# Mixing layer: other block order, selection and softmax by token half between the projection blocks, branches merged block by block

## The reference, cut to what matters

```
proj = rms_norm(h) @ w_in                                  # 1024 x 4808
(q_a, k_a, v_a, q_i, k_i, w_i, gate_b, gate_c, conv_in, g_a, g_b) = split(proj)
    # widths 512, 64, 64, 512, 64, 8, 512, 512, 512, 1024, 1024
q_a, k_a, q_i, k_i = rope(...)                             # 8 heads of 64, one key head each
raw   = einsum(q_i, k_i) * 64 ** -0.5
score = einsum(relu(raw), w_i * 8 ** -0.5); score = -inf where key > query
sel   = top_k(score, 64)                                   # 64 keys per query
p     = softmax(q_a . k_a[sel] * 64 ** -0.5)               # 8 heads
y_a   = (p @ v_a[sel]) @ w_a_out                           # 512 x 1024
z     = causal_conv3(gate_c * conv_in)                     # 512 channels
y_b   = (gate_b * z) @ w_b_out                             # 512 x 1024
merged = sigmoid(g_a) * y_a + sigmoid(g_b) * y_b
h     = h + rms_norm(merged @ w_out)                       # then cross attention to mem
```

## Time and profile before

| | us |
|---|---|
| median of 3 executions | 1478.87 (1474.42 to 1480.12) |
| profiled execution, own time | 1475.65 |
| its span, first to last instruction | 1473.7 |
| TensorE matmuls busy | 1400.1 (95%) |
| VectorE busy | 869.1 (59%) |
| ScalarE busy | 696.3 (47%) |
| mean granted TensorE clock | 0.980 |

### The profile page before, as it was taken

The page is one execution under the profiler, slowest core; times in us unless marked ns, Lnnn a source line. Parts: engine busy times, 40 slices in busy tenths (PEclk is TensorE's granted clock), DMA queues, the critical chain, the costliest instruction groups (busy, mean ns, idle before and its releaser), DMA issues.

```text
span 1473.7 us, 22686 instructions
## 1 busy us (share of the span) xinstructions
PE 1400.1 (95%) x8406; PEld 1151.5 (78%) x8406; DVE 869.1 (59%) x1250; ACT 696.3 (47%) x1094; POOL 39.7 (3%) x41
## 2 busy tenths in 40 slices
PE   6999999889799999999899999999999999899998
PEld 5888878667688878888787688867888887788887
DVE  4555558684664555544775566755555567455554
ACT  5444456455455454434543433315544465464442
POOL 0000000000000000000000000110000011000000
PEclk9999999889899999999898999999999999999999
DMA  8655637335255555565353001203655652255553
GB/s 274 213 171 180 198 119 232 121 128 184 101 175 172 156 168 178 196 203 194 121 172 100 30 3 31 78 29 115 200 183 187 217 177 66 73 181 181 182 188 109
DMA packets 145515, 220.40 MB, mean 150 GB/s; under 512 B 16752, under 2 KB 65150, under 8 KB 145312
## 3 DMA queue, kind: packets, MB, share of 16 engines
q1 hardware_dynamic: 145440, 219.36, 45.5%
HBM read 218.26 MB, written 1.05 MB: 149 GB/s over the span
## 4 chain that ended last, share of the span: by engine, by line
PE 85%; DVE 8%; ACT 4%; issue 2%; POOL 0%; DMA 0%; SPq 0%; ACTq 0%; DVEq 0%
PE gp L287 12%; PE gp L289 11%; PE gp L288 11%; PE acc L287 11%; PE acc L289 11%; PE acc L288 11%; PE tp L904 1%; PE gp L2415 1%; DVE sb_w_lo L276 1%; PE acc L2431 1%; PE acc L2428 1%; ACT sb_w_hi L260 1%; ACT sb_xa_hi L451 1%; ACT sb_arena L401 1%; PE acc L2166 1%
## 5 line engine op out<-in xcount | busy, mean ns | idle before, releaser
L276 DVE TENSOR_TENSOR sb_w_lo<-sb_raw,sb_w_hi 128x1024 fp32r<-128x1024 f32 x380 | 454.5, 1222 | 224.8 <-ACT sb_w_hi L260 222.5
L260 ACT ACTIVATE sb_w_hi<-sb_raw 128x1024 fp32r<-128x1024 f32 x380 | 390.2, 1058 | 222.4 <-PE acc L289 104.8
L287 PE MATMUL gp<-sb_w_hi,sb_xa_hi 128*128 128x512 f32 (+2 forms) x752 | 299.3, 398 | 12.1 <-DVE sb_xa_lo L458 9.9
L289 PE MATMUL gp<-sb_w_lo,sb_xa_hi 128*128 128x512 f32 (+2 forms) x752 | 292.3, 389 | 0.0
L288 PE MATMUL gp<-sb_w_hi,sb_xa_lo 128*128 128x512 f32 (+2 forms) x752 | 292.0, 388 | 0.0
L287 PEld LDWEIGHTS gp<-sb_w_hi,sb_xa_hi 128*128 128x128 f32 x752 | 143.3, 191 | 45.5 <-issue 11.1
L289 PEld LDWEIGHTS gp<-sb_w_lo,sb_xa_hi 128*128 128x128 f32 x752 | 142.9, 190 | 29.5
L288 PEld LDWEIGHTS gp<-sb_w_hi,sb_xa_lo 128*128 128x128 f32 x752 | 143.5, 191 | 27.2 <-issue 0.5
L287 PE MATMUL acc<-sb_w_hi,sb_mid_hi 128*128 128x512 f32 x408 | 159.1, 390 | 0.0
L289 PE MATMUL acc<-sb_w_lo,sb_mid_hi 128*128 128x512 f32 x408 | 158.9, 389 | 0.0
L288 PE MATMUL acc<-sb_w_hi,sb_mid_lo 128*128 128x512 f32 x408 | 158.7, 389 | 0.0
(11 more groups left out here) (410 smaller groups left out, 1785.7 us busy)
## 6 DMA issues: line engine op xcount, KB each, us to landing
sb_raw<-in_ffn_w SPq DMA_DIRECT2D x264, 256.0 KB, 4.3
sb_raw<-in_mlp_w SPq DMA_DIRECT2D x256, 256.0 KB, 2.9
sb_raw<-in_w_in SPq DMA_DIRECT2D x72, 256.0 KB, 3.5
sb_raw<-in_a_w_rkv SPq DMA_DIRECT2D x48, 256.0 KB, 4.0
sb_raw<-in_xattn_w_kv SPq DMA_DIRECT2D x32, 256.0 KB, 3.2
sb_raw<-in_w_out SPq DMA_DIRECT2D x16, 256.0 KB, 5.9
sb_raw<-in_xattn_w_q SPq DMA_DIRECT2D x16, 256.0 KB, 2.9
sb_raw<-in_xattn_w_o SPq DMA_DIRECT2D x16, 256.0 KB, 3.0
```

The lines of the kernel that those rows point to most:

```text
L260: A.e.activation(w_hi[:, s], raw[:, r], ACT.Copy).then_inc(hi_done, 1)
L276: V.e.tensor_tensor(w_lo[:, s], raw[:, r], w_hi[:, s].bitcast(F32), ALU.subtract).then_inc(lo_done, 1)
L287: e.matmul(dst, xh, wh, start=start, stop=False)
L289: return e.matmul(dst, xh, wl, start=False, stop=stop)
```

## The change

In `Mix`:

- The blocks come in another order: k_a v_a and q_i first, then the 200-wide one, then q_a; the rest as before. Splits of a 200-wide chunk now cover 200 columns per row piece, not 512.
- Turns, score pairs, logits, probabilities and values stand between single chunks of the products, not in clumps. The softmax goes by token half: half 0 is complete before the logits of half 1 start.
- The doubled key columns and the first tap of the convolution are made on ScalarE. The causal mask is added with the first head's score; the separate multiply and add, and the work copy, go. The mask needs two operations, not three.
- The values product has the probabilities as the stationary side and 64 value columns moving. The output, not the probabilities, is normalised (`dve_o_rows`), and then turned (`pe_o_turn`).
- w_b_out and w_a_out alternate by column block, and gating, adding and turning of the first 512 columns stand between them. w_out's first block starts on the first quarter of the merged columns.

In the RWKV rows the decay sums stand in two halves behind chunks 1 and 2 of v's block 0, and the second low-rank product in two halves before chunks 0 and 1.

The order of the streams before and now follows at three places. Line numbers of the new file are 1 higher for the helpers (L288 to L290 are the products, L261 and L277 the splits).

TensorE, at the turning of queries and keys: before, one clump between block 5 and block 6 (L1190 turns, L1199 convolution input, L1211 score pairs, L1220 gates).

The diff, cut to its core:

```diff
-            BLOCKS = [(0, 512), (512, 512), (1024, 200), (GATE_C, 512), (CONV_IN, 512), (GATE_B, 512),
+            BLOCKS = [(512, 512), (1024, 200), (0, 512), (GATE_C, 512), (CONV_IN, 512), (GATE_B, 512),
...
+            def pe_values(self, T, t):
+                T.e.wait_ge(self.p_columns, 2 if t == 0 else 6)
+                for head in range(A_HEADS):
+                    for c in range(t + 1):
+                        mm = T.e.matmul(self.side(t)[:, head * HD:(head + 1) * HD], self.p_cols[t][:, c, head, :], self.values[:, c, :],
+                                        start=c == 0, stop=c == t)
+                mm.then_inc(*T.one(self.o))
...
             def pe(self, T):
                 self.proj.pe_first(T, 0, XA, self.bank(0), self.pre.turn, ffn1_post.h_at)
+                self.pe_chunks(T, 1, range(0, 4))
+                self.pe_free(T, 2)
+                self.pe_chunks(T, 2, range(0, 2))
+                T.e.wait_ge(self.roped, 1)
+                self.pe_rows_turn(T, 0, (0, 0), (640, 768))
+                self.pe_chunks(T, 2, range(2, 3))
+                T.e.wait_ge(self.roped, 2)
+                self.pe_rows_turn(T, 1, (0, 1), (896, 0))
+                T.e.wait_ge(self.columns, 1)
+                self.pe_keys_turn(T, 1, 0, 1, 128)
+                self.pe_chunks(T, 2, range(3, 4))
...
+                self.pe_chunks(T, 3, range(2, 3))
+                self.pe_scores(T, range(6, 8))
+                T.e.wait_ge(self.roped, 3)
...
+                self.pe_chunks(T, 8, range(0, 3))
+                T.e.wait_ge(self.yb_f32, 2)
+                self.pe_probs(T, 1, 0, 0, 1)
+                self.pe_probs(T, 1, 0, 1, 0)
+                self.pe_chunks(T, 8, range(3, 4))
...
+                self.yb0.pe(T, 0, yb_x, lambda t: gp[:, t, :], (self.yb_done, 1), (self.taken, 16))
+                self.ya0.pe(T, 0, XB, lambda t: acc[:, t, 0:512], (self.o_done, NT), (self.taken, 18))
+                self.yb1.pe(T, 0, yb_x, lambda t: acc[:, t, 512:1024], None)
+                T.e.wait_ge(self.merged, 2)
+                self.pe_merge(T, 0)
+                self.pe_merge(T, 1)
+                self.ya1.pe(T, 0, XB, lambda t: gp[:, t, :], (self.merged_b, 2))
+                self.pe_out(T, 0)
+                T.e.wait_ge(self.merged, 4)
+                self.pe_merge(T, 2)
+                self.pe_merge(T, 3)
+                self.pe_out(T, 1)
...
             def act(self, A):
...
+                split_hi(A, c[3] + 3)
+                self.act_turned(A, 1, 0, self.queries(4))
+                split_hi(A, c[4] + 1)
+                self.act_twice(A, 2, 1, 128)
...
+                split_hi(A, c[5] + 1)
+                self.act_relu(A, range(5, 6))
...
+                split_hi(A, c[9] + 3)
+                self.act_exp(A, 1, 0)
+                split_hi(A, self.proj.end)
+                self.act_exp(A, 1, 1)
...
             def dve(self, V):
...
+                self.dve_top(V, 0, 0)
+                self.dve_scores(V, range(4, 5))
+                self.dve_top(V, 0, 1)
+                self.dve_scores(V, range(5, 6))
+                split_lo(V, c[5] + 1)
+                self.dve_top(V, 0, 2)
+                split_lo(V, c[5] + 2)
+                self.dve_top(V, 0, 3)
...
             def sp_memory(self, sp):
                 sp.wait_ge(mix.o, NT)
+                sp.wait_ge(mix.yb_f32, 2)
...
+                self.pe_up_rows(T, 0, self.low_a, self.up_a, self.a_up)
+                v.pe_chunk(T, 0, 0, XA, self.bank(4))
+                self.pe_up_rows(T, 1, self.low_a, self.up_a, self.a_up)
+                v.pe_chunk(T, 0, 1, XA, self.bank(4))
+                T.e.wait_ge(*stage(self.taken, 8))
+                self.pe_decay(T, range(0, 4))
+                v.pe_chunk(T, 0, 2, XA, self.bank(4))
+                self.pe_decay(T, range(4, 8)).then_inc(*T.one(self.decay))
+                v.pe_chunk(T, 0, 3, XA, self.bank(4))
...
-                A.e.wait_ge(self.decay, 1)
-                A.e.activation(self.decay_end, gp[:, 0, 0:KT], ACT.Copy).then_inc(*A.one(self.low))
                 self.act_kk_squares(A, 1)
                 A.e.wait_ge(self.kk_ss, 1)
                 for t in range(NT):
                     A.e.wait_ge(self.a_up, t + 1)
                     A.e.activation(rows(1)[:, t, :], acc[:, t, :], ACT.Sigmoid).then_inc(*A.one(self.a_ready))
+                A.e.wait_ge(self.decay, 1)
+                A.e.activation(self.decay_end, tp[:, 0, 0:KT], ACT.Copy).then_inc(*A.one(self.low))
```

More of the change, by code:

```diff
@@ new lines, in pe_pair @@
+            def pe_pair(self, T, n, q0, key, done):
+                t, heads = n // 4, self.TOGETHER[n % 4]
+                for j, head in enumerate(heads):
+                    e = head % 2
+                    q = self.q_cols[e * HD:(e + 1) * HD, q0 + head // 2, t * P:(t + 1) * P]
+                    kk = self.key_cols[e * HD:(e + 1) * HD, key, 0:self.KEYS[t]]
+                    mm = T.e.matmul(self.side(n)[:, j * self.KEYS[t]:(j + 1) * self.KEYS[t]], q, kk, start=True, stop=True)
+                mm.then_inc(*T.one(done))
@@ L1279, in act_take, with act_turned, act_twice @@
                     A.e.activation(dst(t), self.bank(b)(t)[:, 0:self.BLOCKS[b][1]], func, scale=self.pre.rstd(t)).then_inc(*A.one(self.taken))
+            def act_turned(self, A, n, bank, dst):
+                A.e.wait_ge(self.turned, n)
+                A.e.activation(dst, tp[:, bank, 0:dst.shape[-1]], ACT.Copy).then_inc(*A.one(self.columns))
+            def act_twice(self, A, n, slot, at):
+                A.e.wait_ge(self.roped, n)
+                for t in range(NT):
+                    A.e.activation(rows(slot)[:, t, at + HD:at + 2 * HD], rows(slot)[:, t, at:at + HD], ACT.Copy).then_inc(*A.one(self.twice))
@@ L1334, in act @@
-                for t in range(NT):
-                    A.e.wait_ge(self.o, t + 1)
-                    A.e.activation(XB[0][:, 0:4, t * P:(t + 1) * P], self.side(t).rearrange("p (h q) -> p h q", h=4), ACT.Copy).then_inc(*A.one(self.o_hi))
-                split_hi(A, self.ya.end + 4)
-                self.merge.act(A, XA)
-                split_hi(A, self.out.first[0] + 5)
-                xattn.act_memory(A)
-                split_hi(A, self.out.first[0] + 6)
-                xattn.act_mem_columns(A)
@@ L1366, in dve, with dve_max, dve_m_rows @@
+            def dve_max(self, V, t):
+                V.e.wait_ge(*V.last)
+                V.e.tensor_reduce(self.neg_max[:, 8 * t:8 * t + 8], self.logits[t], AX, ALU.max, negate=True).then_inc(*V.one(self.maxed))
+            def dve_m_rows(self, V):
                 V.e.wait_ge(self.taken, 8)
```

685 lines of the change are left out of this document (404 added, 281 removed).

## The result

| | us |
|---|---|
| changed kernel, median of 4 executions | 1444.95 (1444.29 to 1446.45) |
| kernel before, 4 executions beside it | 1478.74 (1474.42 to 1480.12) |
| ratio, 95% interval | 0.9772 (0.9759 to 0.9785) |
| profiled execution of the changed kernel, own time and span | 1445.13, 1443.2 |
| its mean granted clock | 0.994 |

What follows compares the result with a forecast made beforehand. TensorE, 85% of the span, was taken as the bound. Layer: 120.0 + 28.2 + 6.3 + 0.9 = 155.4, 20.0 less; with RWKV 3.5, 1475.65 less 23.5 gives 1452.2, forecast as median 1455, range 1446 to 1469 us.

Steps and rivals of the forecast that it cites:

- clumps: Mixing layer: four stretches of TensorE work other than weight products, 19.5, 13.7, 7.3 and 11.0 us, together 51.5.
- the four places named: Mixing layer waits: index keys' turn 1.3, eighth score pair 0.9, second-half probabilities 1.5, merge of second column half 2.6 us.
- the offset to the median: Whole kernel: the profiled execution lies 3.2 us below the median, so 1452.2 own time became a median forecast of 1455.
- w_out's second chunk: Sign at the mixing layer's end: if the forecast is right, this chunk ends near 376 us.
- two pairs with 256 keys: Sign in the mixing layer's score and logit pairs: 256-key pairs should show near 0.86 us each.
- Rivals 1, 2 and 4: Layer waits move, 1460 to 1469, chance 0.25; clock falls in pieces, 1501, 0.06; selection stays late, gain 8, 1470, 0.05.
- Rival 3: Better than laid out: the layer's four waits vanish, switching is free; up to 30 gained, 1446 to 1451 us, chance 0.12.
- Price of the pieces: Mixing layer: transposes 11.3, narrow pairs 2.9, 256-key pairs 6.9, values 5.3, leaving and re-entering products 1.8; sum 28.2 us.
- Waits, 6.3: Mixing layer: sum in us of the four TensorE waits expected to remain.
- Clock in the layer, 0.9: Mixing layer: the last wait may drop the clock, costing 1.8 us; half was taken, 0.9.
- products: Mixing layer: weight products, only reordered, take 120.0 us of the frame.
- RWKV, 3.5: RWKV rows: splitting decay sums and low-rank products gains 3.5 us, limited by VectorE's row scaling moving 3 to 3.5 earlier.

Runs made afterwards that it cites:

- the kernel with the table loads: Changed kernel with one unused 128x1 sigmoid between the second half's two groups of exponentials, forcing two more ScalarE table loads: 1450.99 us, ratio 0.9812.
- the old tail: Changed kernel with its last part (w_b_out, w_a_out, gates, merge, transposes, w_out) in the old order: 1461.16 us; without a misplaced VectorE scaling, 1457.51 us.

## Why the direction was right and the size too small

In the layer the mechanism was right: clumps go, the pieces run at full clock, four waits stay at the four places named. What failed there is sizes, the price of the pieces above all; in the RWKV rows the limit that was named was the wrong one; and the offset to the median was carried over without a reason. Of the signs, w_out's second chunk ended at 369.3 us, not near 376, and two pairs with 256 keys cost 1.16 together, not 0.86 each. Rivals 1, 2 and 4 did not happen. Rival 3 came nearest in time, but not by its cause: the four waits stayed. The steps:

- **Price of the pieces, 28.2 in the sum.** The 23 gaps between products are 27.7 us, less 4.7 of waits 23.0, plus 1.8 for longer first products, 24.8: 3.4 too dear. The transposes carry 2.3 of it: 88 at 0.129 came from the length of a record of eight, whose last transpose runs out under the next product. By gaps it is 0.79 for eight and 0.35 for four; in all they have 9.0 of the 23.0. The pairs with 256 keys carry 1.1: 0.86 each was taken, two together cost 1.16, because they overlap. The bound from below (0.71) was itself too high: in that row of the kernel before, the second of two pairs started 0.85 us behind the first, so they overlapped only in part. Values (5.2 against 5.3) and narrow pairs (0.74 against 0.72 for two) were right.
- **Waits, 6.3.** 4.7 came. Three were within 0.3 (the third 1.64, so the dearer table load did not come); the merge of the second half was put at 2.6 and took 1.27, because the splits and memory rows held VectorE 0.7 us past the branch's end and not 1.4, and gates, split and adds took 3.6 and not 3.9.
- **Clock in the layer, 0.9.** None in this profile: waits up to 1.64 us left it at 1.00. It is not safe, though: the kernel with the table loads lost it for 3.4 us behind the unchanged wait of 0.63.
- These make 5.9, and products at 120.7 instead of 120.0 take 0.7 back: 5.2, so 25.2 instead of 20.0.
- **RWKV, 3.5.** 4.9. The step that failed is the limit "VectorE's row scaling moves only 3 to 3.5 earlier". Its end moved from 825.5 to 795.6 us, 29.9, of which 26.2 come from what stands before: 3.7, close to the forecast. But TensorE does not start from it: before and after, it waits the same 1.11 us for ScalarE, as the rows below show, and ScalarE waits for TensorE. So all that TensorE saves arrives: 3.6 on the eight records, 0.6 on the products (0.9 was named and set aside) and 0.7 on the decay sums, which the prediction had at nothing.
- **The offset of 3.2.** The profile before was one of the shorter executions, 3.1 below its median, the one after lay at its own. That gives 3.0 of the 10. The repeated profile shows part of the reason: before has more places where the clock may or may not fall, and its first profile had been spared some; another 1.2 us was idle time at full clock. The changed kernel has fewer half-clock stretches, and its runs lay 2.2 us apart. That this is why its profile lay at the median is argued, not shown.
- **The entry** gave 1.0 us that no step had, and 0.5 went again behind the RWKV rows. The 1.0 is luck and not the change: the second profile of the changed kernel has the 3.4 us of half clock at the entry, and that of the kernel before has none.

In own time 5.2 + 1.4 + 1.0 - 0.5 = 7.1; the forecast lay 2.8 above its own time and the measured median 0.2 below the profiled one: 10.1, the whole miss but for rounding. What decides whether a short stretch falls in an execution is left open. The rows for the RWKV step, before and after:

```profile
824.28 0.66 PE L2373 MATMUL gp<-sb_consts,sb_arena 128*128 128x128 f32 x4 [1.11 <-ACT sb_arena L2307]
```

```profile
793.23 0.65 PE L2602 MATMUL gp<-sb_consts,sb_arena 128*128 128x128 f32 x4 [1.11 <-ACT sb_arena L2536]
```

## What to carry to other kernels

Take the price of a small piece from the gaps between the products around it, not from the length of its record, and look whether neighbours overlap. A clump on the bounding engine can be priced by putting it back alone, as the old tail was. Ready work in a wait also kept the clock here, whereas dummy work in the wait only moved the stall. Check which engine the bounding one really waits for before naming a limit. Where before has many half-clock stretches and after will have few, the profiled execution's distance from the median does not carry over; give that its own term.

## What was not expected of the hardware

- Matmuls with 64 rows on different halves of the array ran together: 1.14 us for two pairs against 1.99 on the same half, and starts 0.01 us apart.
- A table load was 1.28 us with 0.01 to 0.02 before the next activation, and two of them in a row added 2.93 us to the wait.
- The same program part kept or lost the clock from one execution to the next: at 525 us 1.00 in one profile and 0.66 in another, worth 1.5 us of products, of which the next wait hid 0.5.
- One execution of the kernel before had TensorE idle for 1.22 us between two transposes of one group, at full clock and with no wait in the profile; the other profile of the same kernel had no such gap.
